# A two-layer trunk on one core: mLSTM queries projected with high and low tokens side by side in one 512-column stream

## The reference

```python
def _hybrid_mixer(h, w_in, ...):
    proj = h @ w_in                                   # (256, 1024) @ (1024, 3592)
    q_m, k_m, v_m, o_m, i_pre, f_pre, q_s, k_s, v_s = _split_columns(proj)
    qk = _causal_conv_silu(jnp.concatenate([q_m, k_m], axis=-1), conv_w, conv_b)
    ...
for layer in range(DEPTH):
    y = _rmsnorm(h, norm_mix_g[layer])
    h = h + _hybrid_mixer(y, w_in[layer], ...)
    ...
```

## Time and profile before

| | us |
|---|---|
| median of 3 runs | 1420.51 (1420.43 to 1420.82) |
| the profiled execution | 1420.79 |
| its span, first to last instruction | 1419.0 |
| PE busy | 1407.2 |
| DVE busy | 1140.3 |
| ACT busy | 1006.6 |

### The profile page before, as it was taken

One profiled execution on the slowest core, in us unless ns is written; L12 is line 12 of the kernel. 1 busy time (PEld: TensorE's weight loads), 2 busy tenths in 40 slices (PEclk: granted clock), 3 DMA queues, 4 the chain that ended last, 5 costly groups with the idle time before them and its releaser, 6 DMA issues.

```text
span 1419.0 us, 19052 instructions
## 1 busy us (share of the span) xinstructions
PE 1407.2 (99%) x7021; PEld 1185.6 (84%) x7021; DVE 1140.3 (80%) x853; ACT 1006.6 (71%) x866; POOL 155.7 (11%) x195
## 2 busy tenths in 40 slices
PE   9999999999999999999999999999999999999997
PEld 8988888889988888888888888888888888888886
DVE  6677544457587888888888988888888888888997
ACT  6877533455887777777777777777777777777775
POOL 2210000000101999400000000000000000002000
PEclk9999999999999999999999999999999999999999
DMA  9745655564544899999999999999999999999993
GB/s 354 267 152 191 215 199 178 176 196 153 182 148 142 324 393 397 387 395 385 366 391 386 366 384 391 379 362 386 380 369 392 392 369 383 391 381 375 394 395 137
DMA packets 188546, 447.04 MB, mean 315 GB/s; under 512 B 7736, under 2 KB 9920, under 8 KB 188496
## 3 DMA queue, kind: packets, MB, share of 16 engines
q1 hardware_dynamic: 184048, 431.12, 83.3%
q0 software_dynamic: 3440, 11.58, 2.2%
q10 hardware_dynamic: 1008, 3.67, 0.6%
HBM read 435.84 MB, written 10.49 MB: 315 GB/s over the span
## 4 chain that ended last, share of the span: by engine, by line
PE 95%; DVE 2%; ACT 1%; DMA 1%; issue 1%; SPq 0%; DVEq 0%; ACTq 0%
PE ps L1755 89%; PE ps L2272 2%; DMA h<-in_x_dram 1%; PE ps L2237 0%; ACT whi L708 0%; PE ps L1787 0%; PE ps L1990 0%; PE ps L2114 0%; PE ps L1879 0%; ACT y L733 0%; SPq L405 0%; PE ps L2241 0%; PE ps L2198 0%; PE ps L1776 0%; PE ps L1881 0%
## 5 line engine op out<-in xcount | busy, mean ns | idle before, releaser
L1168 DVE TENSOR_TENSOR wlo<-raw,whi 128x2048 fp32r<-128x2048 f32 x401 | 917.4, 2291 | 209.4 <-ACT whi L708 208.1
L708 ACT ACTIVATE whi<-raw 128x2048 fp32r<-128x2048 f32 x402 | 771.3, 1919 | 345.7 <-PE ps L1755 338.7
L1755 PE MATMUL ps<-whi,xT_hi 128*128 128x512 f32 (+1 forms) x1232 | 485.9, 394 | 0.3
L1755 PE MATMUL ps<-wlo,xT_hi 128*128 128x512 f32 (+1 forms) x1232 | 479.8, 389 | 0.0
L1755 PE MATMUL ps<-whi,xT_lo 128*128 128x512 f32 (+1 forms) x1232 | 478.7, 389 | 0.0
L1755 PEld LDWEIGHTS ps<-wlo,xT_hi 128*128 128x128 f32 x1232 | 231.2, 188 | 48.7
L1755 PEld LDWEIGHTS ps<-whi,xT_hi 128*128 128x128 f32 x1232 | 231.4, 188 | 46.5 <-issue 1.1
L1755 PEld LDWEIGHTS ps<-whi,xT_lo 128*128 128x128 f32 x1232 | 231.6, 188 | 45.0
L1755 PE MATMUL ps<-whi,hid_hi 128*128 128x512 f32 x536 | 210.2, 392 | 0.0
L1755 PE MATMUL ps<-wlo,hid_hi 128*128 128x512 f32 x536 | 208.8, 390 | 0.0
L1755 PE MATMUL ps<-whi,hid_lo 128*128 128x512 f32 x536 | 208.6, 389 | 0.0
(11 more groups left out here) (288 smaller groups left out, 898.5 us busy)
## 6 DMA issues: line engine op xcount, KB each, us to landing
raw<-in_moe_w_gate_dram SPq DMA_DIRECT2D x112, 1024.0 KB, 7.5
raw<-in_moe_w_up_dram SPq DMA_DIRECT2D x112, 1024.0 KB, 8.0
raw<-in_moe_w_down_dram SPq DMA_DIRECT2D x112, 1024.0 KB, 7.6
raw<-in_w_in_dram SPq DMA_DIRECT2D x25, 1024.0 KB, 5.7
raw<-in_ffn_w_gate_dram SPq DMA_DIRECT2D x10, 1024.0 KB, 5.1
raw<-in_ffn_w_up_dram SPq DMA_DIRECT2D x10, 1024.0 KB, 5.2
raw<-in_ffn_w_down_dram SPq DMA_DIRECT2D x10, 1024.0 KB, 4.9
raw<-in_w_out_dram SPq DMA_DIRECT2D x8, 1024.0 KB, 4.9
```

The costliest lines, as they stand in the source:

```text
L708: act.activation(whi[:, i % NSPLIT, :], raw[:, i % NRAW, :], ACT.Copy).then_inc(hi_ready, 1)
L1168: dve.tensor_tensor(wlo[:, i % NSPLIT, :], raw[:, i % NRAW, :], whi[:, i % NSPLIT, :].bitcast(F32), ALU.subtract).then_inc(lo_ready, 1)
L1755: ins = pe.matmul(acc, lhs, rhs, start=start and m == 0, stop=stop and m == 2, skip_group_check=True)
```

## The change

For QM alone, `query_columns_out` takes the place of `columns_out`. `xT_hi` and `xT_lo` become the two halves of one tensor `xT`, so that for each block of the model the 256 high and the 256 low tokens are 512 adjacent columns. A unit is then two matmuls: 512 columns (high and low tokens) through the high weights, and 256 columns (high tokens) through the low weights. The 512 columns fill a bank, so the four column groups of QM take four banks, `QUERY_BANK = (2, 3, 0, 6)`. Bank 0 is free when VS has been evicted, bank 6 when the gate columns have been copied: PE waits for `rows_out` before the third group and for `gcol` before the fourth, in the first half. DVE adds the two halves of each bank with a `tensor_reduce` (four of them), and multiplies by the tokens' scale in SBUF afterwards. The first two may be read when PE has finished them (`two_units`). KM takes its column groups in the order 2, 3, 0, 1, and PE waits for the third reduction (`units_read`) before group 0.

```diff
-        xT_hi = sb("xT_hi", [P, KC, TT * P], F32R)
-        xT_lo = sb("xT_lo", [P, KC, TT * P], F32R)
+        xT = sb("xT", [P, KC, 2, TT * P], F32R)
+        xT_hi, xT_lo = xT[:, :, 0, :], xT[:, :, 1, :]
...
+                def evacuate_queries():
+
+                    to = qkp[:, 0:4, 3:259]
+                    for c in range(4):
+                        if c == 0:
+                            dve.wait_ge(two_units, l + 1)
+                        elif c == 2:
+                            dve.wait_ge(piece_used, n + 2 * QM + 2)
+                        both_parts = ps[:, QUERY_BANK[c], :].rearrange("p (a t) -> p t a", a=2)
+                        dve.tensor_reduce(to[:, c, :], both_parts, AX.X, ALU.add
+                                          ).then_inc(units_read, 1)
+                    dve.wait_ge(units_read, 4 * l + 4)
+                    dve.tensor_tensor(to, to, token_scale(4), ALU.mult).then_inc(cols_out, 1)
...
+            def unit(bank, kk, w_hi, w_lo, start, stop):
+
+                pe.matmul(ps[:, bank, :], w_hi, xT[:, kk].rearrange("p a t -> p (a t)"), start=start,
+                          stop=False, skip_group_check=True)
+                return pe.matmul(ps[:, bank, 0:256], w_lo, xT_hi[:, kk, :], start=False, stop=stop,
+                                 skip_group_check=True)
...
+            def query_columns_out(l, i, half, between):
+
+                hi, lo = piece(i, 4)
+                for c in range(4):
+                    if half == 0 and c == 2:
+                        pe.wait_ge(rows_out, 3 * l + 1)
+                    elif half == 0 and c == 3:
+                        pe.wait_ge(gcol, 2 * (l + 1))
+                    for k in range(4):
+                        ins = unit(QUERY_BANK[c], 4 * half + k, hi[:, k, c * P:(c + 1) * P],
+                                   lo[:, k, c * P:(c + 1) * P], start=half == 0 and k == 0,
+                                   stop=half == 1 and k == 3)
+                    if half == 1 and c == 1:
+                        ins.then_inc(two_units, 1)
+                    if c == 1 and between is not None:
+                        pair_sums(*between)
+                ins.then_inc(piece_used, 1)
...
+                order = (2, 3, 0, 1) if b == KM else (0, 1, 2, 3)
+                for c in order:
+                    if b == KM and half == 0 and c == 0:
+                        pe.wait_ge(units_read, 4 * l + 3)
...
-                    if c == 1 and between is not None:
+                    if c == order[1] and between is not None:
                         pair_sums(*between)
```

More of the change, by code:

```diff
@@ L54 @@
 OUT_PIECES = (2, 3, 0, 1)
+QUERY_BANK = (2, 3, 0, 6)
 MIX_PIECES = 2 * BLOCKS + 4
@@ L277, in trunk @@
         cols_out = sem("cols_out")
+        two_units = sem("two_units")
+        units_read = sem("units_read")
         rows_out = sem("rows_out")
@@ L1284, in evacuate @@
                     dve.wait_ge(rb_ready, l + 1)
-                    bank = ps[:, 2 * (b % 2):2 * (b % 2) + 2, :].rearrange(
-                        "p b (c t) -> p (b c) t", t=256)
+                    bank = ps[:, 0:2, :].rearrange("p b (c t) -> p (b c) t", t=256)
                     if b == QS:
@@ L1289, in evacuate @@
                                                        ALU.mult, ALU.mult)
-                    else:
-                        g = b - QM
-                        to = ksT[:] if b == KS else qkp[:, 4 * g:4 * g + 4, 3:259]
-                        ins = dve.tensor_tensor(to, bank, token_scale(4), ALU.mult)
+                    elif b == KS:
+                        bank = ps[:, 2:4, :].rearrange("p b (c t) -> p (b c) t", t=256)
+                        ins = dve.tensor_tensor(ksT[:], bank, token_scale(4), ALU.mult)
+                    else:
+                        ins = dve.tensor_tensor(qkp[:, 4:8, 3:259], bank, token_scale(4), ALU.mult)
                     ins.then_inc(cols_out, 1)
+                def evacuate_queries():
[10 more added lines that the diff above has]
+                    dve.tensor_tensor(to, to, token_scale(4), ALU.mult).then_inc(cols_out, 1)
                 def convolve(g, part):
@@ L1399, in mixer @@
                             evacuate(QS)
-                        if half == 1 and b in (QS, KS, QM, KM) and (l, b) != (0, QS):
+                        if half == 1 and b in (QS, KS, KM) and (l, b) != (0, QS):
                             evacuate(b)
+                        if half == 1 and b == QM:
+                            evacuate_queries()
                         if i < 13 and i not in (8, 10):
@@ L1828, in first_columns_out @@
                                      hi[:, k, c * P:(c + 1) * P], lo[:, k, c * P:(c + 1) * P],
-                                     start=half == 0 and k == 0 and c % 2 == 0 and i > 0,
+                                     start=half == 0 and k == 0 and c % 2 == 0,
                                      stop=half == 1 and k == 3, weights_move=False)
@@ L1883, in pair_sums, with columns_out @@
                 ins.then_inc(sum_ps, 1)
-            def columns_out(i, half, bank, between=None):
+            def columns_out(l, b, i, half, between=None):
                 hi, lo = piece(i, 4)
-                for c in range(4):
-                    acc = ps[:, bank + c // 2, 256 * (c % 2):256 * (c % 2) + 256]
+                order = (2, 3, 0, 1) if b == KM else (0, 1, 2, 3)
+                for c in order:
+                    if b == KM and half == 0 and c == 0:
+                        pe.wait_ge(units_read, 4 * l + 3)
+                    acc = ps[:, 2 * (b % 2) + c // 2, 256 * (c % 2):256 * (c % 2) + 256]
                     for k in range(4):
@@ L2028, in mixer @@
                         i = 2 * b + half
-                        out_of = tokens_out if b in (VS, VM, OM) else columns_out
+                        between = (l, i // 2 - 3) if i in (6, 8, 10) else None
                         if b == 0:
@@ L2033, in mixer @@
                             second_columns_out(n + i, 2)
-                        else:
-                            out_of(n + i, half, 2 * (b % 2),
-                                   (l, i // 2 - 3) if i in (6, 8, 10) else None)
+                        elif b == QM:
+                            query_columns_out(l, n + i, half, between)
+                        elif b in (KS, KM):
+                            columns_out(l, b, n + i, half, between)
+                        else:
+                            tokens_out(n + i, half, 2 * (b % 2), between)
                         if i == 2 - l:
```

## The result

The changed kernel takes 1427.24 us (median of 6 runs, 1425.43 to 1427.75) beside 1420.77 us (1420.43 to 1422.20) for the kernel before on the same chip: ratio 1.0043, 95% interval 1.0033 to 1.0053. It is slower, as forecast, but by 6.5 us where 3.9 were forecast, and 0.5 us above the top of the range. The profiled execution took 1427.42 us, 6.63 more than that of before.

The account below looks back on a forecast made before the run. TensorE was taken as the bound, busy 95% of the span. Per layer + 2.13 + 0.10 - 0.27 = + 1.96 us, for two + 3.9 us on the median 1420.51: 1424.4 us; own range 1423.4 to 1425.2, about 8 in 10 within 1423.0 to 1426.7.

Parts of the forecast that it names:

- The unit: In QM, a unit goes from 0.359 to 0.348 us by matmul starts; 24 counting units save 0.27 us per layer.
- The durations: Rival in QM, chance 0.05 that units save far more: by matmul durations 177 ns each, 1416.5 us.
- The sustained spacing of the Trainium skill: In QM, about 131 ns per 512-column matmul, so a unit saves some 108 ns, ending near 1419.8; rival's chance 0.05.
- The wait for bank 0: QM's first half, third group: PE waits for ACT's eviction of VS, 2.13 us plus 0.10 for a longer first step, per layer.
- The reductions, DVE's order and KM's order: Between QM and KM: reductions of 0.69 us cost nothing; slower ones, 1.1 us per layer at most, had chance 0.10.
- A delay is not taken up later: Behind QM, PE's delay reaches the kernel's end one for one; the opposite rival, 1420.5 or 1422.4 us, had chance 0.12.
- The clock falls in the wait: Rival at PE's two 2 us idles in QM: the next 2.8 us of units take twice as long, 1430; chance 0.04.
- the row of 1.00: Earlier trace: granted clock still 1.00 over 2 us of idle PE, 0.50 a microsecond after; cited against a clock fall.
- 0.14 and 0.10 us: At PE's start behind ACT's eviction of VS: 0.14 us from ACT's end to PE's start, 0.10 us longer first step.
- the 13 ns: In QM's units, the low end takes the 256-column step behind a 512 as 106 ns against 120.
- Theory C: Follow-up theory: PE's pause in QM lets the granted clock fall, about 1.5 us per pause on top of the wait.
- Theory D: Follow-up theory: the remainder is late transfers of expert weights (1.9 us) and noise; the clock fall in layer 1 was chance.

Follow-up runs that it names:

- cutting the stream again: Changed kernel with VS evicted ahead of the split, the 512-column matmul cut back into two of 256: 1420.75 us, ratio 1.0003 against the kernel before.
- The wait alone: Kernel before, with PE made to wait for the eviction of VS ahead of column group 2 in QM's first half: 1426.54 us, ratio 1.0046.
- its removal: Changed kernel with ACT evicting VS and copying the gate columns ahead of the split of piece 8: 1420.52 us, ratio 0.9998 against the kernel before.
- the thirty matmuls: Changed kernel with 30 zero matmuls into unused bank 7 ahead of PE's wait for the eviction of VS: 1424.59 us, ratio 1.0031 against the kernel before.
- the first-bank version: Changed kernel with PE waiting only for the first of ACT's two instructions on VS: 1422.69 us, ratio 1.0017 against the kernel before.
- the part-filled wait: Changed kernel with 10 zero matmuls ahead of PE's wait for the eviction of VS, measured twice: 1427.10 us (1.0036) and 1426.74 us (1.0037).
- the keys in order: Changed kernel with KM's column groups in the order 0, 1, 2, 3: 1432.79 us, ratio 1.0095 against the kernel before.

## Why the prediction was right in sign and short in size

**The unit.** Right. 0.353 us a unit (forecast 0.348), and cutting the stream again cost 0.013 us a unit in the traces, too little for the times. The durations in the earlier trace rows overlap and would have given 11.3 us; the starts decided. The sustained spacing of the Trainium skill ("TensorE: Matmul & The Clock Gate", "Back-to-back issue gap"), about 131 ns for 512 columns, is not seen here: no 512-column matmul followed by a 256-column one took less than 0.34 us for both.

**The wait for bank 0.** Right in place, cause and size. PE idled 1.88 us and lost 1.77 us net per layer, where 1.96 was forecast. The sum was 0.2 us too large: PE started 0.05 us behind ACT's end, not 0.14, and the first step of `pair_values(0)` took 0.17 us instead of 0.28 (54.17 to 54.34; before, 52.43 to 52.71). That ACT ended 0.35 us earlier changes nothing, since PE was 0.35 us early too. The wait alone (1.0046) and its removal (0.9998) bound it from both sides. `gcol` cost nothing.

**The reductions, DVE's order and KM's order.** Right: 681 ns each (forecast 0.69 from the 686 ns of the earlier trace rows), one every 0.62 us, no wait of PE for them, and DVE's idle time in front of `soft(2)` covered the rest. KM's order is what buys this, 3.1 us of waiting per layer.

**A delay is not taken up later.** Right: 4.75 us at layer 1 and 4.74 at 1306 us.

**The clock.** Here it failed. The sum and the range have no term for the clock: they put it at nothing. The step was the rival *The clock falls in the wait*, which got 0.04 because "the row of 1.00 speaks against it at this length of wait". The row it rests on the earlier trace rows shows the clock during a pause; what comes behind the pause it can't show. Behind the pauses of 1.9 us the clock fell between 0.2 us before (the wait alone) and about 1.1 us after PE had started again, mostly after. In the five profiled executions with this pause it fell in layer 1 five times and in layer 0 once. Its price was also off: a fall lasts 3.4 us and costs 1.4 to 1.65 us, not 2.8, and not in both layers each time. What the Trainium skill says on the same page under "What's actually happening" (activity is what releases the throttled state) pointed the right way: a filled wait kept the clock, in the profile of the thirty matmuls and by the mean clock of all eight executions. With one fall the sum is 1420.5 + 3.5 + 1.5 = 1425.5 us, which is where the fastest executions lie (1425.24, 1425.43); with two it is 1427.0. Apart from this, the range's own low end does not follow from its terms: leaving out 0.14 and 0.10 us twice gives 1423.9, and the 13 ns give 1423.8, so 1423.4 would need both.

**What was not in the sum at all.** Late transfers of expert weights added 1.87, 1.53 and 0.8 us in the three profiled executions of the changed kernel, and nothing with only the wait added. Before, the longest such wait was 0.9 us. Whether the shift of PE causes them or they come and go is open: with the wait filled by thirty matmuls ACT waited up to 1.6 us for a transfer and PE lost nothing, the first-bank version had no such wait, and the part-filled wait lost 0.5 us once in two. The size of the shift alone does not decide: with the keys in order PE was 11.2 us late and lost nothing there. So Theory C is shown for the falls and for what a filled wait gives back, and Theory D is partly true: of the 6.5 us, 3.5 are the wait, 1.5 to 3.3 the clock, and the rest, up to 1.9, such transfers. In the profiled execution it is one fall and 1.87 us of transfers; how the two share the other executions is not known.

## What to carry to other kernels

Before a wait is moved ahead on TensorE, look up when its releaser ends in its own engine's order: here an eviction stood behind a 1.9 us split, and exchanging the two took the whole loss away. Price a pause of TensorE as its length plus what a slower clock behind it may cost, and read the clock behind the pause, not in it. And judge a wider matmul by the starts of consecutive ones, since their durations overlap.

## What the runs showed of the hardware

- The granted clock fell behind a pause of 1.88 us in 6 of 10 places (layer 1 always, layer 0 once), behind one of 1.3 us in none of 6, behind the 1.55 and 1.24 us that PE waited in the experts of the changed kernel in neither, and behind one of 3.08 us in none of 2. So the length of the pause alone does not decide. What PE does just ahead of and behind it, or where it lies in time, was not separated.
- A fall lasted 3.4 us at 0.50 in all six, and cost 1.4 to 1.65 us. A unit takes 0.64 us in it instead of 0.353.
- A reduction of two halves from PSUM (512 numbers read, 256 written) takes 681 ns on DVE, as the long one in the earlier trace rows does (686), and four in a row take 2.48 us.
- Both profiled executions of one kernel ended 3.6 and 4.4 us later behind DVE's last instruction than that of before, in the final store and in the last wait for PE's sequencer, with five packets on the queue that brings instructions where all others had two.
